# State space exponents masked in PSUM, two heads row-tiled; the norm's statistics a step later; two gate groups behind the stream

## The reference, cut to what matters

```
xbc = silu(causal_dwconv(xbc));  dt = softplus(dt_raw + bias)
cs  = cumsum(dt * a)                                  # per head, 32 heads of 64
L   = exp(where(causal, cs[l] - cs[s], -inf))
cb  = C B^T                                           # per group, 4 groups of 8 heads
y   = (cb * L) @ (x * dt) + d * x                     # chunks are folded into one here
g   = y * silu(z);  y = g * rsqrt(mean(g*g over 512) + eps) * w      # 4 groups
att = sliding window attention with sinks (16 heads of 64)
merged = sigmoid(g_ssd + b0) * (y @ w_ssd) + sigmoid(g_att + b1) * (att @ w_att)
out = merged @ w_out
```

## Time and profile before

| | |
|---|---|
| median of 3 runs | 1676.32 us |
| profiled execution, its own time | 1678.86 us |
| its span, first to last instruction | 1677.0 us |
| TensorE busy | 1616.6 us (96%) |
| VectorE / ScalarE / GpSimd busy | 1113.3 / 921.5 / 199.1 us |
| DMA moved | 266 MB, mean 159 GB/s |
| mean granted TensorE clock | 0.99 |

### The profile page before, as it was taken

The page is one execution under the profiler, slowest core; times in us unless marked ns, Lnnn a source line. Parts: engine busy times, 40 slices in busy tenths (PEclk is TensorE's granted clock), DMA queues, the critical chain, the costliest instruction groups (busy, mean ns, idle before and its releaser), DMA issues.

```text
span 1677.0 us, 31574 instructions
## 1 busy us (share of the span) xinstructions
PE 1616.6 (96%) x12846; PEld 1565.9 (93%) x12846; DVE 1113.3 (66%) x2383; ACT 921.5 (55%) x1990; POOL 199.1 (12%) x194
## 2 busy tenths in 40 slices
PE   7999999999999999999899999899999879999998
PEld 7999999999999999999899999788898769999997
DVE  6555578786747876565388764855368867678862
ACT  5444355564435664365466543657675666466652
POOL 5000000000000000001100000124444652100000
PEclk9999999999999999999999999999999999999999
DMA  8554555555555554643256655644353224545551
GB/s 269 176 176 159 175 170 176 154 174 176 164 168 175 178 176 160 194 151 123 79 178 187 188 168 173 184 126 127 125 178 121 82 76 151 176 151 177 182 177 45
DMA packets 260209, 266.04 MB, mean 159 GB/s; under 512 B 4739, under 2 KB 259025, under 8 KB 260064
## 3 DMA queue, kind: packets, MB, share of 16 engines
q1 hardware_dynamic: 258528, 260.72, 49.4%
q0 software_dynamic: 1536, 3.29, 0.9%
HBM read 262.90 MB, written 1.09 MB: 157 GB/s over the span
## 4 chain that ended last, share of the span: by engine, by line
PE 86%; DVE 7%; ACT 4%; issue 2%; POOL 0%; DMA 0%; SPq 0%; DVEq 0%; ACTq 0%
PE ps L931 53%; PE ps L933 26%; DVE wl L2044 2%; ACT wh L1399 1%; DVE CY L2131 1%; PE ps L716 1%; POOL P L2369 0%; ACT P L1199 0%; DVE CY L2012 0%; PE ps L680 0%; DMA X<-in_x 0%; PE ps L764 0%; PE ps L644 0%; DVE SY L2017 0%; ACT EX L1347 0%
## 5 line engine op out<-in xcount | busy, mean ns | idle before, releaser
L2044 DVE TENSOR_TENSOR wl<-raw,wh 128x512 fp32r<-128x512 f32 x931 | 618.6, 714 | 315.8 <-ACT wh L1399 309.5
L1399 ACT ACTIVATE wh<-raw 128x512 fp32r<-128x512 f32 (+1 forms) x989 | 551.3, 618 | 205.9 <-PE ps L931 205.3
L931 PE MATMUL ps<-XH,wh 128*128 128x258 f32 (+3 forms) x2528 | 641.4, 290 | 8.5 <-ACT XH L1030 4.7
L933 PE MATMUL ps<-XH,wl 128*128 128x258 f32 (+3 forms) x2528 | 633.4, 287 | 0.0
L931 PEld LDWEIGHTS ps<-XH,wh 128*128 128x128 f32 x2528 | 481.2, 190 | 15.5 <-issue 11.0
L933 PEld LDWEIGHTS ps<-XH,wl 128*128 128x128 f32 x2528 | 480.9, 190 | 0.3
L931 PE MATMUL ps<-XL,wh 128*128 128x258 f32 (+3 forms) x2528 | 348.4, 288 | 0.0
L931 PEld LDWEIGHTS ps<-XL,wh 128*128 128x128 f32 x2528 | 325.3, 190 | 2.7 <-issue 1.9
L933 PE MATMUL ps<-HH,wl 128*128 128x272 f32 (+1 forms) x704 | 172.9, 284 | 0.0
L931 PE MATMUL ps<-HH,wh 128*128 128x272 f32 (+1 forms) x704 | 172.9, 284 | 0.0
L933 PEld LDWEIGHTS ps<-HH,wl 128*128 128x128 f32 x704 | 132.6, 188 | 0.0
(11 more groups left out here) (432 smaller groups left out, 2064.1 us busy)
## 6 DMA issues: line engine op xcount, KB each, us to landing
raw<-in_ffn_wg SPq DMA_DIRECT2D x44, 1024.0 KB, 5.3
...
```

The costliest lines, as they stand in the source:

```text
L931: mm = e.matmul(o, hi[:, k, c], xk, start=u.first and part == 0 and k == 0, stop=u.last and end)
L933: e.matmul(o, lo[:, k, c], xk, start=False, stop=False)
L1399: e.activation(wh[u.n % NH][:, c], raw[u.n % NR][:, c], ACT.Copy).then_inc(s_hi, 1)
L2044: e.tensor_tensor(wl[u.n % NR][:, c], raw[u.n % NR][:, c], wh[u.n % NH][:, c].bitcast(F32), ALU.subtract).then_inc(s_lo, 1)
```

## The change: what it does

*Exponents.* The high and low parts of the cumulated sums go into one tile `CSS` on four 32-row strips (high, low, high, low), without the first 14 tokens (402 columns, `NEX`, second chunk first). For each head pair two matmuls of 64 rows, one on rows 0 to 63 and one on rows 64 to 127, put high plus low of the two heads into banks 4 and 5 (`TWO` picks the head). Then one matmul each by the identity adds `MASK` (0 or -1e30, 258 columns). ScalarE takes the exponents of both heads straight from PSUM, four instructions with the bias in `NCT`. VectorE's and ScalarE's clipping, `PCT`, `s_e` and `s_er` are gone; CB is no longer masked. `DTA` is written four times side by side instead of once beside zeros.

*Norm.* `pe_gn` and the copy to `VS` stand at (c-6)%4 = 3 instead of 2. c = 14 and 15 have a step more. The roots of groups 0 and 1 with their table load are taken in c = 14, scale 0 in c = 15; the tail has 11 steps in a new order.

*Groups.* `ga` 2 and 3 go from before `ya` to behind `gs`; their values wait in `TH`, and `ya` 2 and 3 are stored without the gate, which is multiplied in among the `ys` groups. The attention rate is 5.8 for 4.9, that of the `xs` groups 12 for 11.5, that of the tail 10 for 12; GpSimd splits no pieces in the `gs` and moved `ga` groups.

```diff
@@ -25,6 +25,7 @@
...
 MSTRIP = 288
+NEX = 144 + NV
 
@@ -485,11 +488,11 @@
...
     P.queue(6 * 9)
-    P.rate = 4.9
+    P.rate = 5.8
     for j in range(8):
...
         P.group(("z", j), W_IN, KD, Z0 + 256 * j, 2, two(s_z2, 2 * j))
-    for j in range(4):
+    for j in range(2):
         P.group(("ga", j), W_IN, KD, GA0 + 256 * j, 2, two(s_gk, 2 * j))
@@ -503,22 +506,24 @@
...
-        return 3 + (c > 1) + 2 * (c % 2 == 0 and c < 14) + (c > 5 and (c - 6) % 4 < 3)
+        return 3 + (c > 1) + 2 * (c % 2 == 0 and c < 14) + (c > 5) + (c > 13)
...
-            P.credit, P.rate = -4.0, 11.5
+            P.credit, P.rate = -4.0, 12
...
-    P.queue(ssd_steps(14) + ssd_steps(15) + 12)
-    P.rate = 12
+    P.queue(ssd_steps(14) + ssd_steps(15) + 11)
+    P.rate, P.pool = 10, ()
...
+    for j in (2, 3):
+        P.group(("ga", j), W_IN, KD, GA0 + 256 * j, 2, two(s_gk, 2 * j))
...
-    P.rate = 2
+    P.rate, P.pool = 2, (2,)
@@ -725,7 +730,7 @@
...
         e.wait_ge(s_em, 2 * c + 2)
-        for n, (rows_, x0, x1) in enumerate(((128, 0, 272), (128, 272, 416), (16, 0, 16))):
+        for n, (rows_, x0, x1) in enumerate(((128, 144, NEX), (128, 0, 144), (16, 0, 16))):
             for par in range(2):
@@ -737,7 +742,7 @@
...
         e.wait_ge(s_gadd, g + 1)
-        e.wait_ge(s_xd, (9, 13, 16, 16)[g])
+        e.wait_ge(s_xd, (10, 14, 16, 16)[g])
         if g:
@@ -829,8 +834,8 @@
...
-            e.matmul(PS[b][:, 0:272], Bm[:, 0:128], Cm[:, :], start=True, stop=True)
-            e.matmul(PS[b][:, 272:416], Bm[:, 128:256], Cm[:, 128:272], start=True, stop=True)
+            e.matmul(PS[b][:, 144:NEX], Bm[:, 0:128], Cm[:, TS:T], start=True, stop=True)
+            e.matmul(PS[b][:, 0:144], Bm[:, 128:256], Cm[:, 128:272], start=True, stop=True)
@@ -844,35 +849,36 @@
...
                 e.wait_ge(s_xd, c)
-            if c in (9, 13):
-                e.wait_ge(s_vs, (c - 5) // 4)
+            if c in (10, 14):
+                e.wait_ge(s_vs, (c - 6) // 4)
             x = CY[(c // 2) % 4][:, c % 2, :]
...
             yield from idle(c % 2 == 0 and c < 14)
-            for h in (2 * c, 2 * c + 1):
-                b, e_r = 4 + h % 2, identR[:, h:h + 1].to_broadcast([128, 128])
-                if h < 2:
-                    e.wait_ge(s_cbm, 8)
-                    e.wait_ge(s_csh, 1)
-                    e.wait_ge(s_csl, 1)
-                elif h % 2:
-                    e.wait_ge(s_er, h // 2)
-                else:
-                    e.wait_ge(s_e, h // 2)
-                e.matmul(PS[b][:, 0:T], e_r, CSH[:, :], start=True, stop=False)
-                e.matmul(PS[b][:, 0:T], e_r, CSL[:, :], start=False, stop=True).then_inc(s_eb, 1)
-                yield
+            if c == 0:
+                e.wait_ge(s_cbm, 8)
+                e.wait_ge(s_csl, 2)
+            else:
+                e.wait_ge(s_ee, 2 * c)
+            for par in range(2):
+                rows_, h = slice(64 * par, 64 * par + 64), 2 * c + par
+                e.matmul(PS[4 + par][:, 0:NEX], TWO[rows_, h:h + 1].to_broadcast([64, 128]), CSS[rows_, :],
+                         start=True, stop=False)
+            for par in range(2):
+                e.matmul(PS[4 + par][:, 0:258], identR[:], MASK[:], start=False, stop=True).then_inc(s_eb, 1)
+            yield
+            yield
             yield from idle(c % 2 == 0 and c < 14)
-            if c > 5 and (c - 6) % 4 < 3:
-                if (c - 6) % 4 == 2:
+            if c > 5:
+                if (c - 6) % 4 == 3:
                     pe_gn(e, (c - 6) // 4)
                 yield
+            yield from idle(c > 13)
+        pe_ssd_y(e, 14)
+        yield
         pe_gn(e, 2)
-        yield
-        pe_ssd_y(e, 14)
         yield
@@ -880,7 +886,7 @@
...
-        yield from idle(4)
+        yield from idle(3)
@@ -1231,14 +1237,14 @@
...
             e.activation(SY[:], YB[:, 4 * g:4 * g + 4, :], ACT.Square).then_inc(s_gsq, 1)
-        if step == 2:
+        if step == 3:
             e.wait_ge(s_gsum, g + 1)
...
         e.activation(VS[:, g0:g1, :], VS[:, g0:g1, :], ACT.Ln, bias=cc[:, 1:2]).then_inc(s_gl, 1)
-        e.wait_ge(s_gl, 1 if g0 == 0 else 2)
+        e.wait_ge(s_gl, g1 - 1)
         e.activation(VS[:, g0:g1, :], VS[:, g0:g1, :], ACT.Exp, scale=-0.5).then_inc(s_gr, 1)
@@ -1311,10 +1317,10 @@
...
         e.wait_ge(s_dT, 2)
-        e.activation(CSH[:], DCP, ACT.Copy).then_inc(s_csh, 1)
+        e.activation(CSS[:, 0:144], DCP[:, 128:T], ACT.Copy)
+        e.activation(CSS[:, 144:], DCP[:, TS:T], ACT.Copy).then_inc(s_csh, 1)
         e.activation(NCT[:, 0:2, :], src3(CST[:, 0:64], 2), ACT.Copy, scale=-1.0).then_inc(s_dtt, 1)
         e.activation(NCT[0:16, 2, :], CST[0:16, 64:96], ACT.Copy, scale=-1.0).then_inc(s_dtt, 1)
-        e.activation(PCT[:, 0:2, :], src3(CST[:, 0:64], 2), ACT.Copy).then_inc(s_dtt, 1)
         yield
@@ -1334,43 +1340,43 @@
...
             yield
-            h = 2 * c + 1
-            E = EX[h % 4]
-            e.wait_ge(s_eb, h + 1)
-            if h > 3:
-                e.wait_ge(s_y, h - 3)
-            e.activation(E[:, 0:272], PS[5][:, 0:T], ACT.Relu, scale=-1.0, bias=PCT[:, 0, h:h + 1])
-            e.activation(E[:, 272:416], PS[5][:, 128:T], ACT.Relu, scale=-1.0, bias=PCT[:, 1, h:h + 1]).then_inc(s_er, 1)
-            e.wait_ge(s_e, c + 1)
-            e.activation(EX[(h - 1) % 4][:], EX[(h - 1) % 4][:], ACT.Exp).then_inc(s_ee, 1)
-            e.wait_ge(s_er, c + 1)
-            e.activation(E[:], E[:], ACT.Exp, scale=-1.0).then_inc(s_ee, 1)
+            for par in range(2):
+                h = 2 * c + par
+                E = EX[h % 4]
+                e.wait_ge(s_eb, h + 1)
+                if h > 3:
+                    e.wait_ge(s_y, h - 3)
+                e.activation(E[:, 0:144], PS[4 + par][:, 0:144], ACT.Exp, bias=NCT[:, 1, h:h + 1])
+                e.activation(E[:, 144:], PS[4 + par][:, 144:NEX], ACT.Exp, bias=NCT[:, 0, h:h + 1]).then_inc(s_ee, 1)
             yield
             yield from idle(c % 2 == 0 and c < 14)
-            if c > 5 and (c - 6) % 4 < 3:
+            if c > 5:
                 act_gn(e, (c - 6) // 4, (c - 6) % 4)
                 yield
-        act_gn(e, 2, 2)
-        yield
-        e.preload_act_table_set("natural_log_exp_and_others")
-        yield
-        act_gn_root(e, 0, 3)
-        yield
+            if c == 14:
+                e.preload_act_table_set("natural_log_exp_and_others")
+                act_gn_root(e, 0, 2)
+            if c > 13:
+                yield
+        yield
+        act_gn(e, 2, 3)
+        act_gn_root(e, 2, 3)
+        yield
+        act_gn_high(e, 0)
+        yield
+        yield
+        act_gn_high(e, 1)
         yield
...
         yield
-        act_gn_high(e, 0)
-        yield
-        yield
-        act_gn_high(e, 1)
-        yield
-        act_gn(e, 3, 2)
+        yield
+        act_gn(e, 3, 3)
         act_gn_root(e, 3, 4)
...
         yield
-        yield
         act_gn_high(e, 3)
+        yield
         yield
@@ -1565,14 +1571,14 @@
...
-        for j in range(4):
+        for j in range(2):
...
-        e.wait_ge(s_gk, 8)
-        for k in range(KD):
+        e.wait_ge(s_gk, 4)
+        for k in range(4):
@@ -1592,10 +1598,20 @@
...
+        e.wait_ge(s_cz, 24)
+        for j in (2, 3):
+            group(("ga", j))
+            for m in range(2):
+                take(("ga", j), TH[j - 2][:, m, 0:NV], s_gk, m)
+            side.run(groups["ga", j].after)
...
+        e.wait_ge(s_gk, 8)
+        for k in range(4, KD):
+            t = TH[k // 2 - 2][:, k % 2, 0:NV]
+            e.activation(t, t, ACT.Sigmoid, bias=pc("gate_b_2", 8 + k)).then_inc(s_gg, 1)
@@ -1908,18 +1923,30 @@
...
         e.wait_ge(s_nega, 1)
-        e.wait_ge(s_csz, 1)
-        e.tensor_tensor(DTA[:, 0:2, 0:32], src3(PS[6][:, 0:64], 2), AN[:].unsqueeze(1).to_broadcast([128, 2, 32]),
-                        ALU.mult).then_inc(s_cum2, 1)
-        e.tensor_tensor(DTA[0:16, 2, 0:32], PS[6][0:16, 64:96], AN[0:16, :], ALU.mult).then_inc(s_cum2, 1)
-        yield
-        yield
-        yield
-        e.wait_ge(s_dtt, 5)
+        e.tensor_tensor(DTA[:, 0:2, :].rearrange("p i (r h) -> p i r h", r=4),
+                        src3(PS[6][:, 0:64], 2).unsqueeze(2).to_broadcast([128, 2, 4, 32]),
+                        AN[:].unsqueeze(1).unsqueeze(1).to_broadcast([128, 2, 4, 32]), ALU.mult).then_inc(s_cum2, 1)
+        e.tensor_tensor(DTA[0:16, 2, :].rearrange("p (r h) -> p r h", r=4),
+                        PS[6][0:16, 64:96].unsqueeze(1).to_broadcast([16, 4, 32]),
+                        AN[0:16, :].unsqueeze(1).to_broadcast([16, 4, 32]), ALU.mult).then_inc(s_cum2, 1)
+        yield
+        yield
+        yield
+        e.wait_ge(s_dtt, 4)
         e.tensor_tensor(BD[:].rearrange("p (h t) -> p h t", h=32), DCP[0:32, 256:T].unsqueeze(1).to_broadcast([32, 32, 16]),
...
         e.wait_ge(s_csh, 1)
-        e.tensor_tensor(CSL[:], DCP, CSH[:].bitcast(F32), ALU.subtract).then_inc(s_csl, 1)
```

(70 more changed lines are left out.)

41 lines of the change are left out of this document (22 added, 19 removed).

## The result

The changed kernel takes 1672.59 us (median of nine runs, 1671.56 to 1674.17) against 1677.62 us for the kernel before (nine runs on the same chip, 1675.81 to 1681.51). The ratio is 0.9969, its 95% interval 0.9959 to 0.9979: 5.0 us faster, where 10.9 were forecast. The profiled execution took 1673.03 us (span 1671.0), against 1678.86 (1677.0). Lines are those of the changed kernel now: L748 is the group mean (L743 before), L699 the transposes of P (L694), L937/L939 the stream (L931/L933), L856 the first transposes of a step c (L851), L685 the scores (L680), L2399 GpSimd's normalise (L2369).

A forecast was written before the change was run, and what follows sets the result against it. TensorE, busy 96% of the span, was taken to set the end. Terms -11.3 - 3.2 - 0.8 + 1.4 + 3.0 = -10.9 us, from the median 1676.32 to 1665.4 us, range 1660 to 1671, chance 0.51.

The forecast's parts named there:

- price of the change of form: Bias matmuls on TensorE: entering and leaving the 64-row form costs 0.19 us a visit, bounds 0 and 0.19.
- Waits at the mean calls: Group mean in the state space stage: 3.9 of 15.2 us of waits left, gain 11.3 us, bounds 6 and 15.2.
- VectorE's part after y 15: Tail: after TensorE's y 15, VectorE needs 4.6 to 5.7 us to finish the g = 3 sum, low parts included.
- Half clock: TensorE at 1.2 GHz after mean-call gaps: 1.3 of 4.5 us lost work time stays, gain 3.2, bounds 1 and 4.5.
- Small waits: State space stage: new exponents gain only the 0.7 us wait for YB and 0.1 at the CB products, 0.8.
- TensorE work: Exponent block +1.9 us (bounds -1.1, and +5.0 if not side by side), less 0.4 and 0.1 in y and CB: +1.4.
- mask pair: Exponent block on TensorE: two mask matmuls of 258 columns take 0.24 us per c.
- pair of 402 columns: Exponent block: two 64-row bias matmuls run side by side in 0.19 us, 0.38 if not.
- Rival 3: Exponent block: row-tiled fp32r matmuls don't run side by side, +3.1 us on the forecast, 1668.5 us; chance 0.08.
- Attention: Attention loop, denser after two gate groups moved: waits for GpSimd's normalise add 3.0 us, bounds 0 and 6.
- State space stage: All forecast terms but the attention's: the change otherwise worth -13.9 us.
- rival 2: Mean calls: the wait only moves, y 15 and g = 3 wait 9.9 us as before; -3.0, 1673.3 us; chance 0.18.

The follow-up runs named there:

- only_exps: The kernel before with the new exponents alone; norm statistics, tail order and all four ga groups as they were: 1673.14 us, ratio 0.9968.
- full_array: The changed kernel with both bias matmuls on all 128 rows, through weights whose lower half is zero, instead of 64 rows each: 1671.37 us.
- rate55: The changed kernel with 5.5 attention steps a group instead of 5.8: 1669.41 us.
- old_exps: The changed kernel with the exponents as before the change, later norm statistics and the two late gate groups kept: 1680.59 us.

## Why the prediction was wrong, step by step

Forecast -10.9, measured -5.0 us (-6.0 between the profiled executions), which leaves 1672.59 us outside its range of 1660 to 1671. The signs and the waits came mostly as said; what failed is the price of the change of form and the clock behind the attention's waits. By its own steps:

- *Waits at the mean calls, -11.3*: right in kind, -10.0 in size. g = 0, 1 and 2 wait 0.2, 0 and 0 us; g = 3 waits 4.98 where I took 3.1, and 0.8 for y 15. VectorE's part after y 15 was right: from 1365.35 to the end of the sum at 1370.70 are 5.35 us, forecast 4.6 to 5.7. But TensorE's y 15 was done at 1363.1, 2.2 us before VectorE's y 15 began. ScalarE's and then VectorE's timeline in the changed kernel:
```profile
1362.49 1.70 ACT L1253 ACTIVATE YH<-YB,PV 128x258 fp32r<-128x258 f32 x4
1364.09 0.62 ACT L1405 ACTIVATE wh<-raw 128x512 fp32r<-128x512 f32 x1
```
```profile
1364.74 0.69 DVE L2065 TENSOR_TENSOR wl<-raw,wh 128x512 fp32r<-128x512 f32 x1 [1.62 <-ACT wh L1405]
1365.35 0.48 DVE L2056 SCALAR_TENSOR_TENSOR YB<-CY,DC,ps 128x258 f32<-128x258 f32 x1
1365.74 3.75 DVE L2049 SCALAR_TENSOR_TENSOR YL<-YB,PV,YH 128x258 fp32r<-128x258 f32 x8
1369.42 0.67 DVE L2065 TENSOR_TENSOR wl<-raw,wh 128x512 fp32r<-128x512 f32 x1
1370.02 0.68 DVE L2038 TENSOR_TENSOR SY<-SY 128x516 f32<-128x516 f32 x1
```
  The high part of g = 0 holds up ScalarE's high part of a weight, and VectorE stands 1.62 us before that weight's low part with y 15 queued behind it. I had gone through the helpers' norm work in order and not through the stream's pieces between.
- *Half clock, -3.2*: behind the wait of 4.98 us the clock falls, and 2.3 us are lost, not 1.3.
- *Small waits, -0.8*: gone, and the exponents brought far more than this. Pairs of steps c without a wait got longer, from 10.26 and 10.44 us before to 10.81 and 10.80 in only_exps, and still the stage lost 4.8 us, as TensorE's waits in it fell by 7.2 us: VectorE's two passes a step less free the places where TensorE stood for XDT. I had booked that under the statistics, and given the exponents 0.8.
- *TensorE work, +1.4*: this term failed most, by the price of the change of form. The block costs 0.32 us a step more, +5.1, where I took +1.9 and had +5.0 as the bound for another cause. I had a visit at 0.19 us, with that as its upper bound, from what stands ahead of L680 and behind it. Around the block it came out so, 0.20. But another 0.19 lies inside, the load of the pair's weights and the way back, 0.39 in all, and I didn't look inside L680's 1.05 us, where the trace has it too: from its first pair of 272 columns to the second it is 0.33 us, to the third 0.23. The mask pair was right (0.24 and 0.23), and the pair of 402 columns at 0.19, side by side, fits the rows. Rival 3 (not side by side, +3.1) names the right size; full_array at c = 1 speaks against its mechanism.
- *Attention, +3.0*: measured +6.0. The waits came as forecast, +3.3 us. That the clock falls behind them stood in no term, and so was put at nothing; it makes up the other 2.7, by the two windows at 0.66, by rate55, where it stays, and by old_exps, where one of the two stretches stays full and 1.4 us are saved.
- *Rest*: between the attention and c = 0 0.6 us came off; the start differed by 2.8 us, with its cause open.

State space stage: forecast -13.9, measured -8.7. The difference of 5.2 is 3.2 (change of form) + 1.3 (waits) + 1.0 (clock), which makes 5.5. Attention: 3.0 too little. Both misses have one sign; the 3.3 us in the other stretches hid part of them. That the time came out near rival 2's 1673.3 is luck and not its mechanism: the SY waits are 5.0 us, not 9.9.

The Trainium skill (TensorEngine Tiling (Array Packing), Key Properties) says that a change of tiling mode drains TensorE, and the trace agrees: with the weight loads that no longer run ahead it is 0.39 us a visit. Its section Theoretical Speedup gives "Up to 2×" for a dimension of 64 and less; for this pair nothing of it is left, 0.38 us against 0.38, with 0.20 lost around it.
